# Hybrid decoder step on one Trainium2 core: the order of the first forty microseconds rearranged

## The reference

```python
h = rmsnorm(x, norm1_g[l])
z = h @ w_in[l]
u_s5, x_rg, g_rg, q, k, v, o, gi, gf = jnp.split(z, IN_SPLITS, axis=-1)
y1, nr, ni = s5_mixer(u_s5, ...)        # diagonal complex state space model
y2, nh, ncv = rglru_mixer(x_rg, g_rg, ...)  # short convolution, gates, real recurrence
y3, nC, nn, nm = mlstm_mixer(q, k, v, gi + ..., gf + ..., o, ...)
x = x + concatenate([y1, y2, y3]) @ w_out[l]
x = x + moe(rmsnorm(x, norm2_g[l]), router_w[l], ...)
```

```python
step = exp(log_step); mag = exp(lr * step)
ab_re, ab_im = mag * cos(li * step), mag * sin(li * step)
z_re = ((ab_re - 1) * lr + ab_im * li) / (lr * lr + li * li)      # z_im likewise
bb_re, bb_im = cmul(z_re[..., None], z_im[..., None], b_re, b_im)
```

## Time and profile before

| | |
|---|---|
| median of 3 runs | 1098.6 us |
| the profiled execution's own time | 1098.81 us |
| its span, first to last instruction | 1097.0 us |
| PE busy | 1036.5 us (94%) |
| DVE, ACT, POOL busy | 316.1, 197.9, 95.3 us |
| moved by DMA | 429.45 MB, mean 391 GB/s |
| mean granted TensorE clock | 0.993 of full |

### The profile page before, as it was taken

How to read it: one execution, slowest core, us unless ns; L and a number is a source line. 1 busy time by engine, 2 the same in 40 slices (tenths; PEclk the granted TensorE clock), 3 DMA queues, 4 the chain that set the end, 5 groups by cost and what they waited for, 6 DMA issues and landing times.

```text
span 1097.0 us, 13183 instructions
## 1 busy us (share of the span) xinstructions
PE 1036.5 (94%) x5134; PEld 435.2 (40%) x5134; DVE 316.1 (29%) x640; ACT 197.9 (18%) x418; POOL 95.3 (9%) x177
## 2 busy tenths in 40 slices
PE   8999999999999999899889989999899989998997
PEld 5767745334333433343333323333324233433322
DVE  5889456312131212121202112121212121212023
ACT  5543615401110201011000201020102010100002
POOL 6899000000000000000000000000000000000000
PEclk9999999999999999999999999999999999999999
DMA  7533799999999999999999999999999999999995
GB/s 223 194 114 77 260 370 406 427 426 431 430 433 430 430 431 431 431 431 431 434 431 431 431 431 431 431 431 434 431 430 431 431 431 431 431 433 431 424 426 239
DMA packets 62051, 429.45 MB, mean 391 GB/s; under 512 B 12022, under 2 KB 25054, under 8 KB 33342
## 3 DMA queue, kind: packets, MB, share of 16 engines
q1 hardware_dynamic: 60868, 428.16, 93.5%
q10 hardware_dynamic: 1146, 0.79, 0.2%
HBM read 424.68 MB, written 3.67 MB: 390 GB/s over the span
## 4 chain that ended last, share of the span: by engine, by line
PE 55%; DMA 36%; DVE 5%; ACT 2%; issue 1%; SPq 1%; ACTq 0%; DVEq 0%
DMA ring_a<-in_exp_w_dram 27%; PE psum L2405 17%; PE psum L2440 14%; DMA ring_b<-in_exp_w_dram 8%; PE psum L2426 7%; PE psum L2327 3%; PE psum L2158 3%; PE psum L2350 2%; PE psum L1886 2%; PE psum L2449 1%; PE psum L2277 1%; PE psum L2283 1%; DVE rgb L1341 1%; SPq L449 1%; DMA xn<-in_x_prompt_dram 1%
## 5 line engine op out<-in xcount | busy, mean ns | idle before, releaser
L2405 PE MATMUL psum<-ring_a,xg 128*64 128x512 f32 x1200 | 341.8, 600 | 14.4 <-DMA ring_a<-in_exp_w_dram 14.4
L2440 PE MATMUL psum<-ring_a,aT 128*64 128x512 f32 x768 | 217.7, 596 | 8.5 <-DMA ring_a<-in_exp_w_dram 8.2
L2405 PEld LDWEIGHTS psum<-ring_a,xg 128*64 128x64 f32 x1200 | 102.9, 137 | 170.1 <-issue 166.0
L2405 PE MATMUL psum<-ring_b,xg 128*64 128x512 f32 x368 | 152.3, 598 | 7.8 <-DMA ring_a<-in_exp_w_dram 7.8
L1672 DVE TENSOR_TENSOR x<-x,psum 128x512 f32<-128x512 f32 x60 | 41.2, 687 | 367.7 <-PE psum L2350 367.7
L2426 PE MATMUL psum<-ring_a,xg 128*64 128x512 f32 x336 | 103.5, 608 | 14.2 <-DMA ring_b<-in_exp_w_dram 14.2
L2440 PEld LDWEIGHTS psum<-ring_a,aT 128*64 128x64 f32 x768 | 68.0, 137 | 110.2 <-issue 104.3
L2440 PE MATMUL psum<-ring_b,aT 128*64 128x512 f32 x256 | 104.0, 595 | 4.2 <-DMA ring_a<-in_exp_w_dram 2.6
L1760 DVE TENSOR_SCALAR acts<-psum 128x512 f32<-128x512 f32 x32 | 22.0, 688 | 223.3 <-PE psum L2426 207.8
L1045 ACT ACTIVATE acts<-acts 128x512 f32<-128x512 f32 x32 | 20.1, 627 | 296.5 <-DVE acts L1760 296.5
L2405 PEld LDWEIGHTS psum<-ring_b,xg 128*64 128x64 f32 x368 | 43.1, 136 | 75.5 <-issue 63.6
(11 more groups left out here) (508 smaller groups left out, 934.9 us busy)
## 6 DMA issues: line engine op xcount, KB each, us to landing
ring_a<-in_exp_w_dram SPq DMA_DIRECT2D x144, 2048.0 KB, 26.3
ring_b<-in_exp_w_dram SPq DMA_DIRECT2D x46, 2048.0 KB, 24.8
ring_a<-in_w_in_dram SPq DMA_DIRECT2D x4, 2048.0 KB, 8.5
ring_a<-in_w_out_dram SPq DMA_DIRECT2D x2, 2048.0 KB, 9.8
ring_a<-in_w_in_dram SPq DMA_DIRECT2D x3, 1024.0 KB, 5.9
ring_a<-in_state_ml_c_dram SPq DMA_DIRECT2D x4, 512.0 KB, 6.1
out_dram<-ring_a SPq DMA_DIRECT2D x4, 512.0 KB, 6.1
ring_b<-in_exp_w_dram SPq DMA_DIRECT2D x2, 1024.0 KB, 28.5
```

The costliest lines, as they stand in the source:

```text
L2405: m = M(psum[64 * x:64 * x + 64, bk, :], xg[:, k, u, 64 * x:64 * x + 64], w[x][:, 512 * bk:512 * bk + 512], start=False, stop=(k == KD - 1))
L2440: m = M(psum[64 * x:64 * x + 64, 4 + nn, :], aT[:, 2 * j + s, 64 * x:64 * x + 64], w[x][:, 1024 * s + 512 * nn:1024 * s + 512 * nn + 512], ...
```

## The change

1. VectorE copies hT3 as well; its order is hT0, hT2, hT4, hT3, hT5. ScalarE copies only hT1.
2. TensorE starts u0 once the three left halves are copied (`rows_turned(0)`) and waits for the right halves between k = 3 and k = 4. It runs four filler matmuls before, where there were two.
3. The first product L1252 signals `mag_arg`; ScalarE's exp of the magnitude, L751 and L753 wait for that alone, so that the wait for the reduced angle stands behind them, at the sines.
4. SP asks for the five state-row pieces ahead of the gate columns, and for `glw` behind chunk 1.
5. TensorE turns the state rows (`par`) behind step k = 5 of xr0, where they stood between u1 and the gate products; ScalarE copies gp before `bias_piece(0)` and par behind it.

```diff
@@ SP
             for c in range(6):
                 if c == 1:
+                    for x, name in enumerate(("state_s5_re", "state_s5_im")):
+                        sp.dma_start(srow[64 * x:64 * x + 64, :], ...).then_inc(sem("par_loaded"), 16)
+                    sp.dma_start(prow[0:32, :], a["state_ml_n"]...).then_inc(sem("par_loaded"), 16)
+                    sp.dma_start(prow[32:48, :], a["state_rg_h"]...).then_inc(sem("par_loaded"), 16)
+                    sp.dma_start(prow[48:96, :], a["state_rg_conv"]...).then_inc(sem("par_loaded"), 16)
                     sp.wait_ge(sem("wgate_zero"), 1)
                     sp.dma_start(wgate[:, :, 0:2 * H], w_in_cols(GI0, 2 * H)).then_inc(sem("wgate_loaded"), 16)
...
-                    (the same five state pieces)
                     sp.dma_start(gb[:], ...)
                     sp.dma_start(m0[:], ...)
+                if c == 2:
                     sp.dma_start(glw[:], ...)
-                if c == 2:
@@ ScalarE
-            for i in range(2):
-                name = f"hT{2 * i + 1}"
-                await_fill(act, name)
-                for c in range(4):
-                    m = A(hT[:, 4 + c, 128 * i:128 * i + 128], ...)
-                m.then_inc(drained[FILLS[name][0]], 1)
+            await_fill(act, "hT1")
+            for c in range(4):
+                m = A(hT[:, 4 + c, 0:128], ...)
+            m.then_inc(drained[FILLS["hT1"][0]], 1)
...
-            act.wait_ge(*at("angle_reduced", 1))
+            act.wait_ge(sem("mag_arg"), 1)
             A(sm[:, 5, :], sm[:, 2, :], ACT.Exp).then_inc(says_now("mag_ready"), 1)
             A(rsm[:, 0:2], vec("rg_lambda"), ACT.Abs).then_inc(says_now("act_rg"), 1)
             act.wait_ge(*at("act_rg", 1))
             A(g_exp[:, 12:14], rsm[:, 0:2], ACT.Exp, scale=-1.0).then_inc(says_now("act_rg"), 1)
+            act.wait_ge(*at("angle_reduced", 1))
             A(sm[:, 6, :], sm[:, 9, :], ACT.Sin).then_inc(says_now("angle_ready"), 1)
...
             u_out(0)
+            u_out(1)
+            copy_out("gp", gate_parts, bank("gp")[:, 0:T])
             bias_piece(0)
-            u_out(1)
             copy_out("par", parT[:, 0:224], bank("par")[:, 0:224])
-            copy_out("gp", gate_parts, bank("gp")[:, 0:T])
@@ VectorE
-            for k in (0, 2, 4, 5):
+            for k in (0, 2, 4, 3, 5):
...
-            dv(TT(sm[:, 2, :], lr, sm[:, 1, :], ALU.mult))
+            TT(sm[:, 2, :], lr, sm[:, 1, :], ALU.mult).then_inc(sem("mag_arg"), 1)
@@ TensorE
-            keep_warm(2)
-            for k in range(6):
-                b, f = FILLS[f"hT{k}"]
-                pe.wait_ge(drained[b], f + 1)
+            keep_warm(4)
+            def rows_turned(hf):
+                for i in range(len(TILES)):
+                    b, f = FILLS[f"hT{2 * i + hf}"]
+                    pe.wait_ge(drained[b], f + 1)
...
+            rows_turned(0)
             pe.wait_ge(sem("w_in0"), 16)
-            channels("u0", 0, 0)
+            channels("u0", 0, 0, lambda k: rows_turned(1) if k == 3 else None)
             channels("u1", 0, 128)
-            (wait for par_loaded, turn the state rows)
             pe.wait_ge(sem("wgate_loaded"), 16)
             gate_products()
             pe.wait_ge(sem("w_in0_right"), 16)
-            channels("xr0", 0, 256)
+            channels("xr0", 0, 256, state_rows)   # at k == 5: wait for par_loaded, turn the state rows
```

More of the change, by code:

```diff
@@ L469, in _ @@
                 if c == 1:
+                    for x, name in enumerate(("state_s5_re", "state_s5_im")):
+                        sp.dma_start(srow[64 * x:64 * x + 64, :], a[name][0].rearrange("b (j g) p -> (b j) (g p)", g=2)).then_inc(sem("par_loaded"), 16)
+                    sp.dma_start(prow[0:32, :], a["state_ml_n"][0].rearrange("b h k -> (b h) k")).then_inc(sem("par_loaded"), 16)
+                    sp.dma_start(prow[32:48, :], a["state_rg_h"][0].rearrange("b (x n) -> (b x) n", x=2)).then_inc(sem("par_loaded"), 16)
+                    sp.dma_start(prow[48:96, :], a["state_rg_conv"][0].rearrange("b t (x n) -> (b t x) n", x=2)).then_inc(sem("par_loaded"), 16)
                     sp.wait_ge(sem("wgate_zero"), 1)
@@ L738, in _ @@
             act.wait_ge(drained[FILLS["vec"][0]], 1)
-            for i in range(2):
-                name = f"hT{2 * i + 1}"
-                await_fill(act, name)
-                for c in range(4):
-                    m = A(hT[:, 4 + c, 128 * i:128 * i + 128], bank(name)[:, 128 * c:128 * c + 128], ACT.Copy, scale=vec("norm1_g", 4 + c))
-                m.then_inc(drained[FILLS[name][0]], 1)
+            await_fill(act, "hT1")
+            for c in range(4):
+                m = A(hT[:, 4 + c, 0:128], bank("hT1")[:, 128 * c:128 * c + 128], ACT.Copy, scale=vec("norm1_g", 4 + c))
+            m.then_inc(drained[FILLS["hT1"][0]], 1)
             act.dma_start(bias_in[:, 0:512], a["exp_b1"][0].rearrange("e (q n) -> q e n", q=4)).then_inc(sem("bias_loaded"), 16)
@@ L1969, in gate_rows, with state_rows @@
                         ends_fill(m, "grows")
+            def state_rows(k):
+                if k == 5:
+                    pe.wait_ge(sem("par_loaded"), 16 * 5)
+                    await_bank(pe, "par")
+                    TR(bank("par")[:, 0:128], srow[:], ident[:])
+                    ends_fill(TR(bank("par")[:, 128:224], prow[0:96, :], ident[0:96, 0:96]), "par")
+            rows_turned(0)
             pe.wait_ge(sem("w_in0"), 16)
-            channels("u0", 0, 0)
+            channels("u0", 0, 0, lambda k: rows_turned(1) if k == 3 else None)
             channels("u1", 0, 128)
[L1974 to L1977, removed]
             pe.wait_ge(sem("wgate_loaded"), 16)
```

## The result

| | before | after |
|---|---|---|
| median of 20 runs each | 1099.01 us | 1104.07 us |
| lowest and highest | 1098.29, 1100.39 | 1097.36, 1106.62 |
| the profiled execution's own time, its span | 1098.81, 1097.0 us | 1105.35, 1103.6 us |
| TensorE's 32 passes L1888 (before L1886) start at | 119.25 us | 124.55 us |
| from there to the end of the span | 977.8 us | 979.1 us |

The ratio over all runs is 1.0031, with a 95% interval of 1.0021 to 1.0041: slower, by a third of one per cent. The medians alone give 1.0046. The forecast was 1098.2, within 1096.9 to 1099.8. The 20 runs of the changed kernel fall in two groups. Six lie at 1097.36 to 1098.44 us, around the forecast, and thirteen at 1103.39 to 1106.62; one is at 1101.49. The 20 runs of before form one group. Of its 80 runs beside the experiments one lies at 1103.56 and one at 1101.98, and one more, of 2133.81 us, is left out.

The account below looks back on a forecast made before the run. The experts' weight stream behind 130 us was taken to set the pace, so only TensorE's earlier place at 128 us counts. A gain of 0.45 from 1098.6 gives 1098.15, said as 1098.2, range 1096.9 to 1099.8.

Parts of the forecast that it names:

- TensorE's start: At the opening, u0 needs one small copy less and starts at 13.13 instead of 13.46: 0.33 us won.
- The angle, the table load: The sines' table load runs beside the angle, ending at 15.9; VectorE and GpSimd's table both come 1.7 us earlier.
- b's landing: The last b piece lands at 20.5, bounds 19.5 and 22.2; VectorE waits 0.7 and its gain is 0.97 us.
- The rival on this term: The five state-row requests add their whole 2.73 us, L1289 starts at 22.2, the end is 1099.3; chance 0.16.
- par, gp, `bias_piece(0)`, `glw`: State rows and the cast are hidden, by 0.1 and 1.4 us; glw is needed only at 132 us.
- Where it is cut: At the sigmoids, TensorE's fills cut VectorE's gain to 0.45 us, which TensorE then keeps to 128 us.
- the ports: VectorE meets GpSimd differently from 58 to 66.5 us: 1097.0 on the good side, chance 0.17, 1099.4 on the bad, 0.10.
- The stream: The experts' weights behind 130 us are a DMA stream of fixed length, taken as unchanged, that can only begin earlier.
- another time of the stream: Sign of being wrong: the stream behind 130 us takes another time than before although its bytes are the same.

Follow-up runs that it names:

- again_1: The changed kernel, unedited, profiled once more: 1105.10 us.
- again_3: The changed kernel, unedited, profiled a further time: 1099.15 us.
- b_first: The changed kernel with SP's state rows asked for behind c, as before the change: median 1104.46 us, ratio 1.0043.
- warm_gap: The changed kernel with 12 TensorE passes into a still empty bank in the wait before the third S5 bank: median 1100.29 us, ratio 1.0006.
- pool_yields: The changed kernel with GpSimd held back at the last four turns until VectorE's product behind the same scan is done: median 1101.40 us, ratio 1.0010.
- late_half: The changed kernel with GpSimd's last half of the table held back until VectorE is through the RG-LRU scans: median 1097.74 us, ratio 0.9986.
- no_sine: The changed kernel without part 3, so the exp waits for the reduced angle again: median 1100.77 us, ratio 1.0008.
- warm_short: The changed kernel with six TensorE passes into the empty bank in the wait before the third S5 bank: 1101.22 us, ratio 1.0020.

## Why the prediction was wrong

- *TensorE's start*: right. u0 starts 1.95 behind the first hT copy, where it was 2.43: 0.48 won, 0.33 forecast.
- *The angle, the table load*: right. L1268 was forecast for 16.65 and came at 16.10, of which 0.43 is this execution's earlier first copy.
- *b's landing*: right in kind and size. A wait of 0.7 at 20.5 was forecast, 0.99 at 20.19 came. The rival on this term wanted L1289 at 22.2 and is out.
- *par, gp, `bias_piece(0)`, `glw`*: hidden in the profiled execution, as forecast. Where b comes sooner, `par` holds VectorE instead, as the prediction had said for that case: 0.55 us in again_1, 0.92 in again_3, 0.82 in b_first.
- *The failed step* is the one under "Where it is cut": "From here on everything is in series", so that 0.45 us are carried to TensorE's banks and "TensorE goes on 0.45 earlier and keeps that to 128 us". By their times it held in 6 of 20 runs, 1097.36 to 1098.44 against 1098.2, and again_3 shows it held: 0.43 won at TensorE's place. In 13 runs the third bank comes late instead, as their times and three late profiles say; in the profiled one by 1.77, and TensorE's place at 124.55 is 5.30 later. So the median, 1104.07, lies 4.3 us over the upper end of the range.
- The cause was named, as the rival of *the ports*, and mis-sized. It was given 1.2 us either way, 0.75 net on the bad side, and a chance of 0.10. In the profiled execution the stretch from the instruction behind the square root to the first S5 instruction grew from 66.56 - 58.05 = 8.51 to 68.33 - 58.60 = 9.73 us, which is those 1.2. But the table had already taken VectorE's whole lead at 42 to 44 us: the forecast had the cast at 42.8, and it started at 44.32. The prediction counted "five instructions" between 58 and 66.5 us and none before.
- What no rival had is what follows: a longer wait, a half clock for 16 passes (1.7 us), GpSimd caught up through it, and four products at 1.79 (4.0 us on VectorE, of which 2.3 reach TensorE). warm_gap cuts the link from the wait to the clock, and none of its 11 runs is over 1100.71; pool_yields cuts the last, and TensorE reaches its place 2.86 us earlier in its profile; late_half takes away what starts it. Part of it was within reach: the 1.21 us wait was in the trace, and four products of one shape took 0.69 to 0.85. I took an idle TensorE as time that can only be won.
- *The stream* was taken as unchanged. It took 977.3 to 979.1 us in the profiles, without a cause that they show; that alone is more than the 0.45 that was forecast. The prediction had named another time of the stream as a sign of being wrong.
- The chances followed from that: 0.84 within 0.2% of no change, with 0.06 on slower, was far too sure, since the trace of one execution can't show in which of two phases two engines will meet.

The Trainium skill (SBUF — State Buffer, "Who interferes with whom") says that a VectorE instruction with two SBUF inputs contends with a GpSimd one that reads SBUF, and that the one that comes second is held for the whole instruction. The rows agree in kind: the product, two SBUF inputs, starts 0.03 behind GpSimd's 1.41 us product and takes 1.79, where it took 0.56 in pool_yields with GpSimd idle. That is 1.23 more, and GpSimd's product had 1.38 left to run. The copies of 24 columns have one input, and that sentence does not speak of them; their rows show the same, since each ends 0.03 behind the end of GpSimd's product.

**What stays open.** Why one execution of the same program comes to GpSimd's product at 42 us just ahead of it and another just behind is not settled. VectorE waits 0 to 0.99 us for b from one execution to the next, but what it does not wait there it waits for `par`: at L1356 again_1 and again_3 are equally far behind L1268 (18.85 and 18.86 us), and they part only between there and the copies. No run makes VectorE earlier by itself at 26 us, so what that would do to the two groups is untested. Nor is it settled why 1.76 us of idle brought the clock down in no_sine and 2.23 did not in warm_short. That the late group of the 20 timed runs is the same as the late profiles is read from their times and spans; only four executions of the changed kernel, three of them late, have a trace.

## What to carry to other kernels

When a change moves two engines that share work on one memory, don't carry its shift through their overlap as a constant: price each short instruction at both of its durations, and ask for several executions, since one trace shows one phase only. An idle stretch of TensorE is not free to grow: a few us more can cost its clock, and engines that depend on each other can lock in the wrong phase behind it. The remedy here was to hold GpSimd off for 3.7 us of VectorE's critical stretch.

## What the runs showed of the hardware

- Two VectorE scans of 128x288 take 3.04 us beside GpSimd's 128x512 products, and 1.55 with GpSimd idle. A copy of 128x3 takes 1.04 when it starts 0.02 behind such a product, and 0.17 to 0.20 otherwise.
- A VectorE product of 128x384 with two SBUF inputs takes 0.56 with GpSimd idle (pool_yields) and 1.79 started 0.03 behind a GpSimd product of 1.41 us. Since GpSimd is released by the scan in front of it, the collision came four times in a row, at intervals of 6.2 us.
- The granted clock went to 0.50 behind a wait of 1.76 us in one program and stayed at 1.00 behind 2.23 us in another. A fall showed in four or five windows of one us below 1.00 in five profiles, and in eight windows in again_1.
- Twelve passes that are thrown away, 3.07 us, took the spread of the changed kernel from 9.3 us (20 runs) to 1.1 us (11 runs of another series).
- An execution's time fell in one of two groups 5 us apart, on one core, with the same bytes moved.
